# PEER key scores from query weights times subkeys, made in the first stage and kept in DRAM

## The reference, cut to what matters

```python
q = (hf @ w_q).astype(jnp.float32).reshape(t, PEER_HEADS, 2, PEER_HALF)     # 8 heads, 2 halves of 128
sc = jnp.einsum('thpc,hpnc->thpn', q, subkeys.astype(jnp.float32))          # 128 subkeys per half
s1, i1 = lax.top_k(sc[:, :, 0], PEER_TOPK)                                  # 16 best of each half
```

## Time and profile before

| | |
|---|---|
| median of 3 runs | 2739.71 us (2739.37 to 2740.38) |
| the profiled execution | 2741.34 us, span 2739.5 us, mean granted clock 0.991 |
| TensorE busy | 2670.2 us (97%) |
| VectorE busy | 2323.9 us (85%) |
| ScalarE, GpSimd busy | 1272.3 us (46%), 1437.7 us (52%) |
| first stage | to 129.27 us |
| `mix_out` | 468.6 to 580.90 us |
| `score` | 580.90 to 797.03 us |

### The profile page before, as it was taken

The page is one execution under the profiler, slowest core; times in us unless marked ns, Lnnn a source line. Parts: engine busy times, 40 slices in busy tenths (PEclk is TensorE's granted clock), DMA queues, the critical chain, the costliest instruction groups (busy, mean ns, idle before and its releaser), DMA issues. The chain is left out here.

```text
span 2739.5 us, 40163 instructions
## 1 busy us (share of the span) xinstructions
PE 2670.2 (97%) x14923; PEld 2362.3 (86%) x14923; DVE 2323.9 (85%) x4158; ACT 1272.3 (46%) x2551; POOL 1437.7 (52%) x937
## 2 busy tenths in 40 slices
PE   7999899989999999999999999999999999999998
PEld 6777566679999999999999999997888888888887
DVE  4297897449989989988989898877999999999997
ACT  4244443233322223998899999863222222222222
POOL 1122321014248886666666666553666666666652
PEclk9999899999999999999999999999999999999999
DMA  4110101233249886999999999999999999999995
GB/s 125 41 39 24 62 1 39 77 99 98 67 154 304 301 297 219 378 391 398 400 388 409 401 390 405 393 389 375 387 388 388 388 388 388 386 387 388 387 386 210
DMA packets 333059, 762.67 MB, mean 278 GB/s; under 512 B 24176, under 2 KB 159344, under 8 KB 330304
## 3 DMA queue, kind: packets, MB, share of 16 engines
q0 software_dynamic: 111104, 403.02, 38.9%
q1 hardware_dynamic: 221040, 353.68, 36.0%
q10 hardware_dynamic: 720, 3.41, 0.3%
HBM read 667.73 MB, written 92.27 MB: 277 GB/s over the span
## 5 line engine op out<-in xcount | busy, mean ns | idle before, releaser
L2144 POOL DMA_INDIRECT v_rows<-in_peer_v,row_numbers x336 | 535.6, 1594 | 328.4 <-DVE y_rest L2217 194.0
L1775 PE MATMUL expert_pre<-h2T,wq_then_uT_hi 128*128 128x320 f32 x4096 | 669.3, 312 | 2.3 <-PEq L1454 2.3
L1889 POOL DMA_INDIRECT u_rows<-in_peer_u,row_numbers x384 | 534.4, 1392 | 241.9 <-DVE row_weights L1909 162.4
L1775 PEld LDWEIGHTS expert_pre<-h2T,wq_then_uT_hi 128*128 128x128 f32 x4096 | 609.4, 188 | 2.4 <-issue 2.4
L2274 PE MATMUL expert_out<-v_hi,w_hi 128*128 128x512 f32 x1280 | 499.8, 390 | 11.9 <-DVE w_lo L2195 11.3
L1909 DVE CUSTOM_DVE_ANT_0 u_rows<-u_rows,h_rows_kept 128x1024 f32<-128x1024 f32 x384 | 487.4, 1297 | 23.5 <-DMA u_rows<-in_peer_u,row_numbers 22.7
L2274 PE MATMUL expert_out<-v_lo,w_hi 128*128 128x512 f32 x1280 | 498.7, 390 | 0.0
L2274 PE MATMUL expert_out<-v_hi,w_lo 128*128 128x512 f32 x1280 | 498.7, 390 | 0.0
L2217 DVE SCALAR_TENSOR_TENSOR y_rest<-v_rows,row_weights,y_rest 128x1024 f32<-128x1024 f32 x256 | 327.3, 1283 | 19.3 <-DMA v_rows<-in_peer_v,row_numbers 18.6
L1775 PE MATMUL expert_pre<-h2T,wq_then_uT_lo 128*128 128x320 f32 x2048 | 342.0, 309 | 0.0
L1775 PEld LDWEIGHTS expert_pre<-h2T,wq_then_uT_lo 128*128 128x128 f32 x2048 | 310.9, 188 | 0.0
(11 more groups left out here) (350 smaller groups left out, 4001.7 us busy)
## 6 DMA issues: line engine op xcount, KB each, us to landing
pick_memory<-in_peer_v SPq DMA_DIRECT2D x128, 512.0 KB, 12.9
wq_then_u<-in_peer_u_turned SPq DMA_DIRECT2D x86, 512.0 KB, 8.2
pick_memory<-acts_dram SPq DMA_DIRECT2D x128, 320.0 KB, 12.3
acts_dram<-expert_acts SPq DMA_DIRECT2D x124, 320.0 KB, 6.1
gates_dram<-pick_memory SPq DMA_DIRECT2D x19, 2048.0 KB, 11.3
pick_memory<-gates_dram SPq DMA_DIRECT2D x58, 448.0 KB, 14.3
third_u<-in_peer_u_turned SPq DMA_DIRECT2D x42, 512.0 KB, 8.3
wq_then_u<-in_peer_wq SPq DMA_DIRECT2D x32, 512.0 KB, 4.0
```

What stands on the lines that cost most here:

```text
L1775: last = nc.tensor.matmul(pre[:, (2 * c + half) % 4, 0:WIDTH], part[:, c % 2, k], m.h2T[:, t, k, HALVES[half]], start=n == 0, stop=n == le ...
L1889: pool.indirect_dma_start(rows[:, k % RING], None, table, bass.IndirectOffsetOnAxis(ap=m.row_of[:, f, slot:slot + 1], axis=0)).then_inc(fe ...
L2144: pool.indirect_dma_start(rows[:, k % ROW_RING], None, d.peer_v, bass.IndirectOffsetOnAxis(ap=m.row_of[:, f, slot:slot + 1], axis=0)).then ...
```

## The change

Since q times a subkey is h2 times (w_q times the subkey), the product of the query weights and the subkeys is made once, in the first stage: 16 products (`KEY_HEADS`, one for each half head) of 128 x 128 subkeys by 128 x 1024 turned weights, as 8 float32 matmuls into a slot of `turned`, each after an item of `project`. ScalarE keeps the high part, VectorE the low part, and SP stores both in DRAM (2 x 512 KB for each). `joined_hi` and `joined_lo` are single buffers. In `score` a pass loads both parts for both halves of a head (2 MB) and makes the scores of a token tile by 24 matmuls of 256 columns, tokens stationary. There are 8 passes over the row tiles (pass 0 is in `mix_out`) and 8 over the dense ones. The second of the two buffers for the keys is the tile of the output weights' high part, so it is loaded once the last fox product has been read. The query weights are no longer split, the queries no longer copied, the subkeys no longer turned on the chip. The host hands over `peer_wq` and `peer_subkeys` turned.

```diff
+        KEY_HEADS, JOIN_FROM = 2 * d.PH, 2
+        subkeys, wq = sb("subkeys_turned", [P, KEY_HEADS, P]), sb("wq_turned", [P, 2, D])
+        joined_hi, joined_lo = sb("joined_hi", [P, D], F32R), sb("joined_lo", [P, D], F32R)
...
+                def load_turned(x):
+                    if x >= 2:
+                        sp.wait_ge(joined_made, x - 1)
+                    sp.dma_start(wq[:, x % 2], d.peer_wq_turned[x]).then_inc(keys_in[x % 2], 16)
+
+                def store_joined(x):
+                    for part, (ready, of) in enumerate(((joined_kept, joined_hi), (joined_split, joined_lo))):
+                        sp.wait_ge(ready, x + 1)
+                        sp.dma_start(d.joined[part, x // 2, :, x % 2], of[:].bitcast(F32)).then_inc(joined_stored, 16)
+
+                sp.dma_start(subkeys[:], d.peer_subkeys_turned).then_inc(keys_in[0], 16)
                 for i in range(2, CHUNKS + 2):
                     sp.wait_ge(m.w_lo_done, i - 1)
                     load_weights(sp, d, m, i)
+                    for x in (2 * i - 4, 2 * i - 3):
+                        if x < KEY_HEADS:
+                            load_turned(x)
+                        if 2 <= x < KEY_HEADS + 2:
+                            store_joined(x - 2)
+                for x in (KEY_HEADS - 2, KEY_HEADS - 1):
+                    store_joined(x)
+                sp.wait_ge(joined_stored, 32 * KEY_HEADS)
...
+                def keep_joined(x):
+                    if 0 <= x < KEY_HEADS:
+                        act.wait_ge(joined_made, x + 1)
+                        if x:
+                            act.wait_ge(joined_stored, 32 * x)
+                        A(joined_hi[:], turned[:, x % 2].rearrange("p k n -> p (k n)"), ACT.Copy).then_inc(joined_kept, 1)
...
+                    keep_joined(n - 1 - JOIN_FROM)
                 for half in range(2):
                     n = len(items) + half
                     act.wait_ge(product_done, n + 1)
                     A(m.forget[:, half * HALF:(half + 1) * HALF], product[0:d.FH, n % 4], ACT.Identity, bias=fbias[:]
                       ).then_inc(product_read, 1)
+                    keep_joined(n - 1 - JOIN_FROM)
+                keep_joined(KEY_HEADS - 1)
...
+                def low_joined(x):
+                    if 0 <= x < KEY_HEADS:
+                        dve.wait_ge(joined_kept, x + 1)
+                        if x:
+                            dve.wait_ge(joined_stored, 32 * x)
+                        v.tensor_tensor(joined_lo[:], turned[:, x % 2].rearrange("p k n -> p (k n)"),
+                                        joined_hi[:].bitcast(F32), ALU.subtract).then_inc(joined_split, 1)
+
+                for n, (i, half) in enumerate(items):
+                    if half == 1:
+                        split_low(i + 2)
+                    low_joined(n - 1 - JOIN_FROM)
+                for x in range(len(items) - 1 - JOIN_FROM, KEY_HEADS):
+                    low_joined(x)
...
+                def join_keys(x):
+                    if x == 0:
+                        pe.wait_ge(low_done, NT)
+                    pe.wait_ge(keys_in[x % 2], 16 * (x // 2 + 1 + (x % 2 == 0)))
+                    if x >= 2:
+                        pe.wait_ge(joined_split, x - 1)
+                    for k in range(KT):
+                        last = nc.tensor.matmul(turned[:, x % 2, k], wq[:, x % 2, k * P:(k + 1) * P], subkeys[:, x],
+                                                start=True, stop=True)
+                    last.then_inc(joined_made, 1)
...
                     multiply(n)
+                    join_keys(n - JOIN_FROM)
...
+                load_joined(sp, d, m, 0)
...
+                    if b == NT - 1:
+                        load_joined(sp, d, m, 1)
...
+                def first_scores(tiles):
+                    if tiles[0] == 0:
+                        pe.wait_ge(m.joined_in[0], 32)
+                        pe.wait_ge(dve4, max(lowered(F - 1), added(NT - 1, LRU_READ)))
+                    for t in tiles:
+                        last = scores_of_tile(nc, m, m.front, 0, t, t)
+                    if tiles[-1] == F - 1:
+                        last.then_inc(m.scored, 1)
...
+def load_joined(sp, d, m, s):
+
+    for part in range(2):
+        sp.dma_start(m.joined[s % 2][part].bitcast(F32), d.joined[part, s % d.PH].rearrange("p a (k n) -> p a k n", n=P)
+                     ).then_inc(m.joined_in[s % 2], 16)
+
+
+def scores_of_tile(nc, m, banks, s, t, place):
+
+    KT, F = m.d.D // P, m.ROWS_TILES
+    hi, lo = m.joined[s % 2]
+    columns = lambda part, k: (m.h2_of_rows[:, part, k, t * P:(t + 1) * P] if t < F else
+                               m.h2T[:, part, k, (t - F) * P:(t - F + 1) * P])
+    to = banks[:, place // 2, place % 2 * 2 * P:(place % 2 + 1) * 2 * P].rearrange("p (a n) -> p a n", a=2)
+    terms = [(part, of, k) for part, of in ((0, hi), (1, hi), (0, lo)) for k in range(KT)]
+    for n, (part, of, k) in enumerate(terms):
+        last = nc.tensor.matmul(to, columns(part, k), of[:, :, k], start=n == 0, stop=n == len(terms) - 1)
+    return last
...
+                for s in range(2, PASSES):
+                    sp.wait_ge(scored, s - 1)
+                    load_joined(sp, d, m, s)
...
-                for s in range(3, 2 * HP):
-                    pool.wait_ge(hi_done, s + 1)
-                    pool.tensor_tensor(wlo[:, s % 2], w[:, s % 2], whi[:, s % 2].bitcast(F32), ALU.subtract
-                                       ).then_inc(lo_done, 1)
...
+                for s in range(1, PASSES):
+                    pe.wait_ge(m.joined_in[s % 2], 32 * (s // 2 + 1))
                     if s >= 2:
                         pe.wait_ge(scores_read, s - 1)
-                    for t in tiles_of(s):
-                        last = nc.tensor.matmul(score_ps[:, s % 2, t], qT[:, s % 2, t * P:(t + 1) * P],
-                                                keysT[:, s % HP], start=True, stop=True)
+                    for place, t in enumerate(tiles_of(s)):
+                        last = scores_of_tile(nc, m, banks_of(s), s, t, place)
...
+                    A(to[:, h % ring].rearrange("p a t n -> p t a n"), made.rearrange("p (t a n) -> p t a n", a=2, n=NK),
+                      ACT.Copy).then_inc(scores_read, 1)
+
+                for s in range(PASSES - 2):
+                    scores_out(s)
+                scores_out(PASSES - 2)
                 act.wait_ge(m.u_in[0], 16)
-                act.wait_ge(query_done, items_through(2 * HP - 2))
-                A(whi[:, 0], w[:, 0], ACT.Copy).then_inc(m.uhi_done, 1)
-                scores_out(2 * HP - 1)
+                A(uhi[:, 0], u[:, 0], ACT.Copy).then_inc(m.uhi_done, 1)
+                scores_out(PASSES - 1)
```

191 lines of the change are left out of this document (45 added, 146 removed).

## The result

The changed kernel takes 2754.95 us as a median of 6 runs (2751.89 to 2761.25), the kernel before 2739.41 beside it (2737.74 to 2740.38). The ratio is 1.0057, with a 95% interval of 1.0046 to 1.0068: slower by 15.5 us, where 2.7 were forecast. The time lies at the upper edge of the range of 2733 to 2755 us, not in the middle of it.

A forecast was written before the change was run, and what follows sets the result against it. TensorE was taken to bound the first stage, TensorE and VectorE both to fill the score stage. First stage +37.6, mix_out +1.9 and score stage -36.8 gave +2.7 on 2739.7, about 2742 us; range 2733 to 2755.

The forecast's parts named there:

- Score stage: TensorE: Score stage: 1464 matmuls of 256 columns at 0.120 us make it 179.3 us instead of 216.1, -36.8 us.
- rival (b): Score stage: keys of the row passes land late, 10 us instead of 8.4; 2748 us, chance 0.12.
- (d): Score stage: 256 column matmuls pace at 0.111 us, VectorE holds the gain to about 7; 2735 us, chance 0.07.
- Score stage: VectorE: Score stage: VectorE's chain falls from 189.1 to about 170 us without GpSimd's subtractions and ends ahead of TensorE.
- Rival (c): Score stage: VectorE's chain stays 189 us and ends last, 12.3 us worse; 2754 us, chance 0.06.
- Products of keys: First stage: fifteen key products at 1.7 us each move the last forget product by 25.5 us.
- I cost both at nothing: First stage: single buffers (cycle 5.1 of 7.15 us) and weight loads behind stores cost TensorE no waiting.
- The tail: First stage's end: copies, subtractions and store landings of the last two key products follow the forget product, +10.1 us.
- The clock after the tail: After the first stage: TensorE restarts at a low clock after 9.5 us idle, +2.0 us.
- rival (e): After the first stage: TensorE's slow start is hidden and the tail's stores land sooner; 2737 us, chance 0.10.
- `mix_out`: End of mix_out: later last turning, and last x2 store behind 2 MB of keys, +1.9 us (0.95 to 2.7).
- Rival (a): First stage: stores set the pace, landing in 5 us instead of 2.6; 2750 us, chance 0.17.

The follow-up runs named there:

- all_three: tail_buffers plus the earlier loads of loads_ahead, with the last x2 store in mix_out asked for ahead of the keys of pass 1; 2739.39 us, ratio 0.9998.
- tail_buffers: Changed kernel with two buffers each for high and low parts, key products 11 to 15 made earlier, each copied behind its own item; 2738.14 us, ratio 0.9998.
- loads_ahead: Changed kernel with the next chunk's w_in columns asked for ahead of an iteration's second pair of stores instead of behind it; 2750.85 us, ratio 1.0041.
- after: The changed kernel itself, in its first profiled execution (2757.5 us); median 2754.95 us, ratio 1.0057.
- after_again: The changed kernel run and profiled once more, unaltered; 2756.77 us, ratio 1.0055 to the kernel before.
- first_part_alone: Kernel before with only the change's first stage: all 16 key products made, split and stored but never read; 2792.53 us, ratio 1.0194.
- buffers_only: Changed kernel with two buffers each for high and low parts of the joined keys, key products left in place; 2747.29 us, ratio 1.0027.
- two_stores: Changed kernel without the stores of 14 of the 16 key products, all still made and split, every head scored with the first pair; 2745.67 us, ratio 1.0021.
- moved_only: Changed kernel, single buffers kept, last key products made ahead of both forget products and each copied behind its own item; 2742.96 us, ratio 1.0013.
- scratch_last: Changed kernel with the 16 MB scratch for joined keys allocated behind the activations and gates instead of ahead of them; 2753.01 us, ratio 1.0054.
- two_products: Changed kernel without 14 of the 16 key products and their loads, splits and stores, every head scored with the first pair; 2710.07 us, ratio 0.9894.
- gpsimd_back: Changed kernel with 13 unused GpSimd subtractions of 128 x 1024 added in the score stage, one behind each of passes 0 to 12; 2756.29 us, ratio 1.0063.

## Why the prediction was wrong, step by step

**Score stage: TensorE** held. 36.3 us against 36.8; matmuls of 256 columns start every 0.120 us (in all_three a pass of 72 takes from 623.18 to 631.82). No gap stands between passes, which excludes rival (b); the pace excludes (d).

**Score stage: VectorE** held as well: 167.8 us for 170. Rival (c) is excluded.

**Products of keys**: mis-sized. 1.7 us were taken between 1.65 and 1.79; 1.83 is the price (tail_buffers: 29.3 for 16), so 27.5 instead of 25.5 for the fifteen. The 1.7 itself came true: from the first record of a key product to the next large matmul it is 1.70 us (loads_ahead, 89.72 to 91.42). What was left out stands behind it: the sixteen matmuls of 512 columns that follow take 3.76 us from first start to the seventeenth, where they took 3.63 in the earlier trace rows. +2.0 us.

**"I cost both at nothing"** is the step that failed. TensorE waits 3.7 us in after's first stage (2.6 of them as visible idle time, the rest inside records), 6.4 in after_again, 10.0 in first_part_alone (from the first key product to the end of the last forget product, less the 109.5 us that this takes in loads_ahead; the last number with the low clock in it). I summed the cycle of one buffer (5.1 of 7.15 us), and separately noted that weight loads come later, but did not put the two in one loop: the weight split stands ahead of the key copy in ScalarE's program, the key copy feeds the next key product and also waits for the last store, and the next weight columns are asked for behind its own stores. Each run that opens this loop at one place takes all the waits away: loads_ahead at the loads, buffers_only at the copy's wait for a store, two_stores at the stores, and moved_only by copying an item earlier. ScalarE's waits for weight columns fall from 19.7 us to 0, 6.8, 1.9 and 0. The condition that I gave, a store that lands 2 us later, was the wrong one; the stores landed in 2.7 (high) and 3.5 us (low), the columns in 5.7.

**The tail**: 11.6 us against 10.1. Right in mechanism from copy 14 on: from its start to the next stage it was 10.44 us (160.90 to 171.34), some 10.4 in the forecast. The 1.5 stand ahead of it: copy 14 was to follow the forget copy at once and waited 1.45 us for the low part of product 13, which the same loop had made late. In loads_ahead that wait is gone and the tail is 10.0 us. two_stores, buffers_only and moved_only show the chain and each way out of it.

**The clock after the tail**: 1.7 for 2.0; some 0.3 of it stands in moved_only and tail_buffers too, which have no long idle time there. So rival (e), a cheap restart and a shorter tail, is excluded.

**`mix_out`**: 3.5 to 4.0 in six profiles, 5.4 to 5.9 in four, against 1.9. The late store was foreseen and is 1.6 us (turning of tile 7 to the next start 5.65 us, against 4.01 in the earlier trace rows). Not foreseen: the fox matmuls pace at 0.231 to 0.234 us instead of 0.227 (a tile takes 13.33 us for 13.21), some 0.9 us in all; TensorE has 24 matmuls of 0.120 at b = 6, where 24 of 384 columns filled the wait for VectorE, and now idles 1.7 to 2.07 us; and in those four profiles the clock fell behind an idle time of 2.07. The last turning was to come 0.95 us later, and did by about 1 (from turning 6 to turning 7 12.24 us in scratch_last, 11.21 before). "At b = 6 the work gets shorter and TensorE waits for VectorE anyway" counted the idle time as free and forgot the clock.

**The last stage**: nothing was forecast, 4.5 us came in this execution and in half of those like it. The cause is open.

The sum: +2.0 (products), +3.7 (waits), -0.7 (a start at the higher clock), +1.5 (tail), -0.3 and -1.0 (`recur`, `attend`), +3.5 (`mix_out`), +0.5 (score), -0.3 and +4.5 (the expert stages) are the 13.4 us between 2.7 and 16.1. The waits and the tail's 1.5, 5.2 us together, are the one failed step; the last stage's 4.5 may be chance, since half of such profiles lack them. No large term was wrong. That the median still lies just inside the range is luck: its upper part stood for rivals (a) to (c), and none of them came as described. Rival (a) named the right place and nearly the right time, 2750, but by another mechanism: stores do not set the pace by themselves, since in loads_ahead all of them are made and TensorE does not wait. The chance of 0.5 for "within 0.2%" took the errors of the small terms to be as likely below as above; but a term costed at nothing could only go up.

## What to carry to other kernels

Where two large terms cancel, the forecast is the sum of the small ones: list each that was costed at nothing, and write it as one loop with its neighbours in the same engine's program and in the same queue. A store to DRAM that nobody waits for belongs ahead of the stage's last work that hides it: making the last key products ahead of the two forget products, which were there already, and copying each an item earlier gave back 13 us of the first stage without a buffer (moved_only, 1.0013 times the kernel before). With the buffers too the kernel takes what the one before takes (0.9998); that the buffers add anything to this is not shown. The score stage's 36 us are paid with 29 for the key products and 2 to 4 in `mix_out`; what is left is too little for these times to tell.

## What the runs showed of the hardware

- TensorE's clock after an idle time of about 2.07 us is not settled: seven profiles had that wait ahead of the turning of tile 6, and in four the granted clock fell to the lower level for 3.4 us (`mix_out` 117.7 to 118.2), in three it did not (116.1 to 116.3).
- A key product of 16 records at 0.112 us costs 1.83 us between 512 column matmuls: 1.70 to the next large matmul's start, and 0.13 in the sixteen behind it.
- One kernel's executions are spread over 3 to 6 us for the kernel before, 9 for the changed one, 8 for tail_buffers, 2.3 for two_products (4 runs). In the changed kernel the waits of the first stage alone differed by 2.7 us between two profiles of it.
- GpSimd's own subtractions were held up too: two of the 13 in gpsimd_back took 4.4 and 4.6 us instead of 2.4.
